# Two layers of a hybrid decoder: attention's output norm taken into the next head's first stage, and a projection dealt out between scores

## The reference

```
xn = rms_norm(x, norm_mix);  columns of every mixer = xn @ w_in
A retention        S_t = gamma_h S + k v;          o = q S
B gated recurrence S_t = diag(f_t) S + k v;        o = S q      (f per channel)
C delta rule       S_t = g (I - beta k k') S + beta k v
D differential attention over the prompt, or over a paged cache + 8 tokens
o_A..o_C = head_rms_norm(o) * silu(gate)
o_D      = head_rms_norm(o) * (1 - lam_init)
h = x + (sum_b sigmoid(G_b xn) * (o_b @ W_b)) @ w_out
y = h + product-key experts(rms_norm(h))
```

## Time and profile before

| | us |
|---|---|
| median of 3 runs | 6727.6 (6712.52 to 6736.32) |
| the profiled execution | 6737.32 |
| its span | 6735.6 |
| PE busy | 6265.5 (93%) |
| DVE busy | 3591.6 (53%) |
| ACT busy | 2141.3 (32%) |
| granted TensorE clock, mean | 0.958 |

### The profile page before, as it was taken

How to read it: one execution, slowest core, us unless ns; L and a number is a source line. 1 busy time by engine, 2 the same in 40 slices (tenths; PEclk the granted TensorE clock), 3 DMA queues, 4 the chain that set the end, 5 groups by cost and what they waited for, 6 DMA issues and landing times. The chain is left out here.

```text
span 6735.6 us, 109246 instructions
## 1 busy us (share of the span) xinstructions
PE 6265.5 (93%) x42728; PEld 5868.9 (87%) x42728; DVE 3591.6 (53%) x6661; ACT 2141.3 (32%) x3172; POOL 0.7 (0%) x6
## 2 busy tenths in 40 slices
PE   8998988979999989999989989889799999899999
PEld 6776768979999989999967767689799999899999
DVE  3444353337778865555434443533377888655554
ACT  2333333222234442222223333332222344422222
POOL 0000000000000000000000000000000000000000
PEclk9999988989999999999999999889899999999999
DMA  2212112224346655444322121122243466554543
GB/s 101 65 49 75 56 42 73 84 88 120 113 130 188 182 187 195 167 178 166 135 88 67 48 75 56 44 73 82 88 123 114 128 187 187 186 193 166 179 165 136
DMA packets 494389, 804.29 MB, mean 119 GB/s; under 512 B 81652, under 2 KB 302836, under 8 KB 475892
## 3 DMA queue, kind: packets, MB, share of 16 engines
q1 hardware_dynamic: 494116, 800.67, 37.4%
HBM read 616.20 MB, written 186.72 MB: 119 GB/s over the span
## 5 line engine op out<-in xcount | busy, mean ns | idle before, releaser
L1625 PE MATMUL ps<-xh,wh 128*128 128x288 f32 x4608 | 1376.5, 299 | 44.3 <-DVE wl L1841 44.3
L1625 PE MATMUL ps<-xl,wh 128*128 128x288 f32 x4608 | 1361.9, 296 | 0.0
L1625 PE MATMUL ps<-xh,wl 128*128 128x288 f32 x4608 | 1357.1, 295 | 0.0
L2041 PE MATMUL ps<-gh,vh 128*128 128x320 f32 (+1 forms) x4096 | 894.9, 300 | 73.2 <-DVE vl L2106 73.2
L1625 PEld LDWEIGHTS ps<-xh,wh 128*128 128x128 f32 x4608 | 867.2, 188 | 47.5 <-DVE wl L1841 45.2
L2041 PE MATMUL ps<-gl,vh 128*128 128x320 f32 (+1 forms) x4096 | 884.6, 298 | 0.0
L2041 PE MATMUL ps<-gh,vl 128*128 128x320 f32 (+1 forms) x4096 | 884.3, 297 | 0.0
L1625 PEld LDWEIGHTS ps<-xh,wl 128*128 128x128 f32 x4608 | 868.4, 188 | 0.0
L1625 PEld LDWEIGHTS ps<-xl,wh 128*128 128x128 f32 x4608 | 867.2, 188 | 0.0
L2106 DVE TENSOR_TENSOR vl<-vr,vh 128x512 fp32r<-128x512 f32 x512 | 353.2, 690 | 690.3 <-ACT vh L2061 690.0
L2041 PEld LDWEIGHTS ps<-gh,vh 128*128 128x128 f32 x4096 | 634.6, 191 | 86.2 <-issue 74.3
(11 more groups left out here) (374 smaller groups left out, 9175.7 us busy)
## 6 DMA issues: line engine op xcount, KB each, us to landing
raw<-in_u SPq DMA_DIRECT2D x256, 512.0 KB, 4.0
vr<-in_v SPq DMA_DIRECT2D x512, 256.0 KB, 2.9
activated<-go SPq DMA_DIRECT2D x256, 288.0 KB, 4.3
coefficients<-wt SPq DMA_DIRECT2D x36, 2048.0 KB, 9.3
gb<-activated SPq DMA_DIRECT2D x64, 1152.0 KB, 5.9
wb<-coefficients SPq DMA_DIRECT2D x64, 1152.0 KB, 8.3
wr<-in_w_cm SPq DMA_DIRECT2D x104, 512.0 KB, 4.5
wm<-in_w_merge SPq DMA_DIRECT2D x32, 768.0 KB, 4.2
```

The costliest lines, as they stand in the source:

```text
L1625: last = nc.tensor.matmul(out, wp[:, slot, k, :], xp[:, k, cols], start=(k == 0 and wp is T.wh and xp is T.xh), stop=(k == KD - 1 and wp i ...
L2041: last = nc.tensor.matmul(out, vp[:, x % 4, m * P:(m + 1) * P], gp[:, row, col:col + size], start=begins, stop=False, skip_group_check=True)
```

## The change

In words:

- `attention_stage` of heads 0, 1 and 2 no longer has the sum of squares, the root and the multiplication. ACT writes the square of the output to `T.late_sq` and then copies the output to `T.late` (both new tiles in SBUF), and the stage ends there. Head 3 keeps the old order.
- `retention_stage` of heads 1, 2 and 3 gets this work. PE sums the squares into banks 2 and 3 before anything else, and it waits for `late_mean` before the state products, which write those banks. ACT makes Ln and Exp before it takes unit 0. DVE multiplies `T.late` by gain and root into the branch buffer between `sc_ready` and the state updates.
- `hgrn_stage`, all heads: unit 4 goes into PE's queue as two halves, ahead of the scores of tiles 2 and 3. Unit 5 goes as four quarters: one ahead of the scores of tile 4, one after the transposes, one after the wait for the last mask and one after the state products. Unit 5 now uses bank 5 instead of bank 1, so PE waits for `taken` 6 before the outputs. The test whether the bank is free stands before the first part of a unit alone.

```diff
@@ -151,17 +151,19 @@
 FIRST_SLOTS = ((0, 1), (1, 1), (2, 1))
 
 
-def pe_ahead(nc, pe, T, s, slots, u, b, banks=1):
+def pe_ahead(nc, pe, T, s, slots, u, b, banks=1, first=0, count=KD):
     c, a = divmod(u, 2)
     slot, loads = slots[c]
-    if a == 0 and loads:
-        pe.wait_ge(s["w"][slot], 16 * loads)
-    if u >= banks:
-        pe.wait_ge(s["taken"], u - banks + 1)
-    for k in range(KD):
+    if first == 0:
+        if a == 0 and loads:
+            pe.wait_ge(s["w"][slot], 16 * loads)
+        if u >= banks:
+            pe.wait_ge(s["taken"], u - banks + 1)
+    for k in range(first, first + count):
         last = nc.tensor.matmul(bank(T, b)[:, 0:HALF], T.wr[:, slot, k, :], T.xn[:, k, a * HALF:(a + 1) * HALF],
                                 start=(k == 0), stop=(k == KD - 1))
-    last.then_inc(s["ahead"], 1)
+    if first + count == KD:
+        last.then_inc(s["ahead"], 1)
 
 
 def load_tile(sp, T, s, l, h, column, slot, after=0):
@@ -475,12 +477,12 @@
     sp.dma_start(T.s_in[:], state[l, :, h].rearrange("s k v -> k s v")).then_inc(s["s_loaded"], 16)
 
 
-def retention_stage(nc, T, l, h, slot):
+def retention_stage(nc, T, l, h, slot, late_slot):
 
     q, k, g = T.ret
     hq, hf, hg, hneg = T.hgrn
     qd = T.wk[:, 2, :]
-    with stage(nc, *W_SEMS, *AHEAD, "small_in", "scored", "turned", "sc_ready", *FINISH, *STATES) as (block, s):
+    with stage(nc, *W_SEMS, *AHEAD, "small_in", "late_sum", "late_mean", "late_root", "scored", "turned", "sc_ready", *FINISH, *STATES) as (block, s):
         s["w"] = [s["w0"], s["w1"], s["w2"], s["w3"]]
 
         @block.sync
@@ -494,6 +496,8 @@
 
         @block.tensor
         def _(pe):
+            if late_slot is not None:
+                wide_product(nc, T, 2, lambda k: T.ones, lambda k: T.late_sq, 1).then_inc(s["late_sum"], 1)
             for t in range(TILES):
                 last = nc.tensor.matmul(tile(bank(T, 4, NP_), t), tile(k, t), tile(q, t), start=True, stop=True)
             last.then_inc(s["scored"], 1)
@@ -501,6 +505,8 @@
                 last = nc.tensor.transpose(tile(bank(T, 6, NP_), t), tile(k, t), T.ident)
             last.then_inc(s["turned"], 1)
             pe_ahead(nc, pe, T, s, HGRN_SLOTS, 0, 1)
+            if late_slot is not None:
+                pe.wait_ge(s["late_mean"], 1)
             pe_state_products(nc, pe, T, s, lambda t: T.vt[:, t, 0:P])
             pe_ahead(nc, pe, T, s, HGRN_SLOTS, 1, 1)
             pe.wait_ge(s["sc_ready"], 1)
@@ -523,6 +529,11 @@
                 else:
                     act_take(nc, act, T, s, u, b, hg, ACT.Silu)
 
+            if late_slot is not None:
+                act.wait_ge(s["late_sum"], 1)
+                nc.scalar.activation(T.rs, halves(T, 2), ACT.Ln, bias=T.eps, scale=1.0 / P).then_inc(s["late_mean"], 1)
+                act.wait_ge(s["late_mean"], 1)
+                nc.scalar.activation(T.rs, T.rs, ACT.Exp, scale=-0.5).then_inc(s["late_root"], 1)
             take(0)
             take(1)
             act_square(nc, act, T, s)
@@ -541,6 +552,11 @@
                                     ALU.mult).then_inc(s["keys_ready"], 1)
             link(nc.vector.tensor_tensor(qd, q, T.hc[:, H_QD:H_QD + NP_], ALU.mult))
             nc.vector.tensor_tensor(T.sc, bank(T, 4, NP_), T.hc[:, H_RM:H_RM + NP_], ALU.mult).then_inc(s["sc_ready"], 1)
+            if late_slot is not None:
+                dve.wait_ge(s["late_root"], 1)
+                link(nc.vector.scalar_tensor_tensor(out=two(T.br[:, late_slot, :].rearrange("p a n -> p (a n)")),
+                                                    in0=two(T.late), scalar=T.cols[:, 8:9], in1=T.rs,
+                                                    op0=ALU.mult, op1=ALU.mult))
             dve_prompt_states(nc, dve, T, s, link, T.hc[:, H_GT:H_GT + TILES])
             dve_sample_states(nc, dve, T, s, link, T.hc[:, H_G8:H_G8 + DEC_B])
             dve.wait_ge(s["small_in"], 16)
@@ -608,6 +624,7 @@
                 n = 1 + (LEVELS if t < 4 else 3)
                 b = 2 * (t % 2)
                 if t >= 2:
+                    pe_ahead(nc, pe, T, s, GDN_SLOTS, 4 + t // 4, 4 + t // 4, 2, *((0, 4), (4, 4), (0, 2))[t - 2])
                     pe.wait_ge(s["masked_"], t - 1)
                 for i in range(n):
                     lhs, rhs = (ke[0], q) if i == 0 else (ke[i - 1], qf[i - 1])
@@ -617,10 +634,12 @@
             for t in range(TILES):
                 last = nc.tensor.transpose(tile(bank(T, 6, NP_), t), tile(ke[LEVELS if t < 4 else 3], t), T.ident)
             last.then_inc(s["turned"], 1)
-            pe_ahead(nc, pe, T, s, GDN_SLOTS, 4, 4, banks=2)
+            pe_ahead(nc, pe, T, s, GDN_SLOTS, 5, 5, 2, 2, 2)
             pe.wait_ge(s["masked_"], TILES)
+            pe_ahead(nc, pe, T, s, GDN_SLOTS, 5, 5, 2, 4, 2)
             pe_state_products(nc, pe, T, s, vt)
-            pe_ahead(nc, pe, T, s, GDN_SLOTS, 5, 1)
+            pe_ahead(nc, pe, T, s, GDN_SLOTS, 5, 5, 2, 6, 2)
+            pe.wait_ge(s["taken"], 6)
             pe.wait_ge(s["sc_ready"], TILES)
             pe.wait_ge(s["st_ready"], 1)
             pe.wait_ge(s["s_loaded"], 16)
@@ -633,7 +652,7 @@
         def _(act):
             act.wait_ge(s["lb_in"], 1)
             nc.scalar.activation(T.lb[:, 0:2], T.lb[:, 0:2], ACT.Exp).then_inc(s["lb_exp"], 1)
-            take = lambda u: act_take_gdn(nc, act, T, s, u, 4 + u % 2 if u < 5 else u % 2)
+            take = lambda u: act_take_gdn(nc, act, T, s, u, 4 + u % 2 if u < 6 else u % 2)
             for r in range(LEVELS):
                 act.wait_ge(s["level_v"], r + 1)
                 if r:
@@ -1262,7 +1281,8 @@
                                             at[:, i * NS + b * DEC_T:i * NS + (b + 1) * DEC_T], start=False,
                                             stop=(b == DEC_B - 1 and i == PAGES - 1))
             last.then_inc(s["o_ready"], 1)
-            pe_finish(nc, pe, T, s)
+            if not more:
+                pe_finish(nc, pe, T, s)
 
         @block.scalar
         def _(act):
@@ -1320,8 +1340,14 @@
             nc.scalar.copy(at[:, 0:PAGES * NS], bank(T, 2)[:, 0:PAGES * NS]).then_inc(s["s_at"], 1)
             nc.scalar.copy(at[0:NS, PAGES * NS:(PAGES + 1) * NS],
                            bank(T, 2)[0:NS, PAGES * NS:(PAGES + 1) * NS]).then_inc(s["s_at"], 1)
-            act_square(nc, act, T, s)
-            act_root(nc, act, T, s)
+            if more:
+                act.wait_ge(s["o_ready"], 1)
+                nc.scalar.activation(T.late_sq, bank(T, 4, N), ACT.Square)
+                nc.scalar.copy(T.late, bank(T, 4, N)).then_inc(s["o_squared"], 1)
+                act.wait_ge(s["o_squared"], 1)
+            else:
+                act_square(nc, act, T, s)
+                act_root(nc, act, T, s)
 
         @block.vector
         def _(dve):
@@ -1382,12 +1408,13 @@
             nc.vector.tensor_scalar(diag[0][0][:, 0:NS], dc[:, C_STK:C_STK + NS], sm(0, 0), None, ALU.mult
                                     ).then_inc(s["diag_ready"], 1)
             link(nc.vector.tensor_tensor(gain, T.ph[:, Q_DN:Q_DN + 1], T.pl[:, L_OL:L_OL + 1], ALU.mult))
-            dve_finish(nc, dve, T, s, link, gain, slot, None)
+            if not more:
+                dve_finish(nc, dve, T, s, link, gain, slot, None)
 
 
 def head(nc, T, l, h, more):
 
-    retention_stage(nc, T, l, h, br_slot(0, h))
+    retention_stage(nc, T, l, h, br_slot(0, h), br_slot(3, h - 1) if h else None)
     hgrn_stage(nc, T, l, h, br_slot(1, h))
     gdn_stage(nc, T, l, h, br_slot(2, h), more)
     attention_stage(nc, T, l, h, br_slot(3, h), more)
@@ -2197,6 +2224,8 @@
                     T.ph = sb(sub, "ph", [P, PH_W])
                     T.vt = sb(sub, "vt", [P, TILES, 3 * P])
                     T.st = sb(sub, "st", [P, 5, P])
+                    late = sb(sub, "late", [P, 2, N])
+                    T.late, T.late_sq = late[:, 0, :], late[:, 1, :]
                     T.s_in = sb(sub, "s_in", [P, DEC_B, P])
                     T.s_new = sb(sub, "s_new", [P, DEC_B, P])
                     T.kt = sb(sub, "kt", [P, TILES, P])
```

## The result

The changed kernel took 6678.47 us, the median of four runs (6672.0 to 6690.07), and the kernel before 6730.46 beside it (6712.52 to 6736.32). The ratio is 0.993, with a 95% interval of 0.9918 to 0.9942; it is worked out over the runs and is not the quotient of the two medians (0.9923). The forecast was 6685, so 43 us less than before, where 52 were measured. The profiled execution took 6679.22 us with a span of 6677.6.

A forecast was written before the change was run, and what follows sets the result against it. PE was taken as the bound, with a serial chain at attention's end and DVE's masking ahead of the recurrence's keys copy. The norm move's 26 us plus the dealt units' 17 gave 43 less, 6685 us, range 6662 to 6708.

The forecast's parts named there:

- Part 1, the chain: Attention's end, six transitions: removing the path from square to barrier saves 5.3 us per transition.
- the sum of squares at 1.0 us: Retention's start: PE's added sum of squares costs only its full-clock time, 1.0 us per transition; the high end is 1.9.
- Nothing on PE but its order: Eight recurrence stages: no PE work is added or removed; 12 of unit 5's 16 instructions move into PE's pauses.
- DVE not delayed: Recurrence: scores of tiles 2 and 3 still reach DVE in time, with margins of 0.8 and 0.6 us.
- Part 2 at full clock, 9.3 us: Recurrence: the stretch from the keys' copy to the square shrinks from 11.60 to 9.3 us at full clock.
- 38 us without falls: Recurrence: gain if the clock held in all eight stages, 74 us against 112.5 from keys' copy to square.
- Falls, 2.5 of 8 at 8.3 us each: Recurrence: two or three of eight stages lose PE's clock, each costing 8.3 us, leaving 17 us of gain.
- The clock held in all eight: Rival, recurrence: split idle time never costs the clock; gain 64 us, so 6664; chance 0.13.
- Retention paid: Rival: sum of squares stays at low clock and DVE's multiplication is exposed; whole gain 32, so 6696; chance 0.09.
- the 1.9 of the rival: Retention: price in us of PE's sum of squares per transition if it stays at the low clock throughout.
- Eight falls: Rival's extreme, recurrence: the clock is lost in every stage; 8 us slower, so 6736; chance 0.03.
- scores were late: Rival, recurrence: scores of tiles 2 and 3 reach DVE late; 1 us late leaves 35, so 6693; chance 0.05.

The follow-up runs named there:

- experiment 4: Changed kernel with the last quarter of unit 5 also ahead of the state products: 6660.0 us, ratio 0.9902 to the kernel before.
- experiment 6: Changed kernel with three unused products in the entry stage of each layer, meant to start all heads 1.5 us later: 6675.32 us, one run.
- Part 1 alone: Kernel before with only attention's norm move, the recurrence keeping its old order: 6710.31 us, ratio 0.9971 to the kernel before.
- experiment 3: Changed kernel with two unused products in each of PE's two pauses before the state products: 6659.55 us, ratio 0.9905 to the kernel before.
- experiment 9: Changed kernel with four unused products at the end of attention of heads 0 to 2: 6679.08 us, ratio 0.9931 to the kernel before.
- Experiment 5: Changed kernel run once more with no edit: 6675.84 us, ratio 0.9918 to the kernel before.
- experiment 8: On experiment 4's kernel, the next head's first recurrence unit moved from retention into PE's waits at attention's end: 6638.34 us, ratio 0.987 to the kernel before.
- experiment 10: On experiment 8's kernel, the recurrence's sum of squares halfway through unit 6 and ACT's root before units 6 and 7: 6633.79 us, ratio 0.9858 to the kernel before.

## Why the prediction was right, and where it was not

- *Part 1, the chain.* Forecast 5.3 us per transition; the timeline shows 7.83 before and 2.08 after, 5.75. Right, and a little small: the copy overlaps the square by 0.1 us, and from the copy's end to PE's first product it is 0.9 us where 1.14 was taken.
- *Part 1, the sum of squares at 1.0 us.* About right: per head with the late norm retention is 1.07 us longer with the move alone, 0.5 in the profile of the changed kernel, where the clock came back 0.8 us sooner than before, and 1.4 in experiments 4 and 6. The state products did not wait for Ln, and DVE's multiplication stayed hidden with 1.71 us to spare. Part 1 alone is 30 us in the two stages of one profiled execution (26 forecast) and 15 in the median of ten runs. The profiled execution is the second fastest of the ten, whose spread is 27 us; what the slower ones lost was not profiled.
- *"Nothing on PE but its order", DVE not delayed.* Right in every trace.
- *Part 2 at full clock, 9.3 us.* Right (9.45), and 38 us without falls is 37 in experiment 3. The pauses were forecast at 1.3 and 1.1 us and are 1.47 and 0.81. Head 3 escaped the forecast, which had 2.66 us of pause for all: there it was 3.05 before, and both its stages fell; after, it is 1.84.
- *Falls, 2.5 of 8 at 8.3 us each.* This term was mis-sized for the profiled execution: four falls at 9.5, so 38 us in place of 21. Over the six profiled executions with this order of units it was 4, 3, 1, 1, 1 and 2, so 2.0 of 8. The chance was well sized, the price some 13% too low. Head 0 against head 1 shows where: state products 0.9 and 1.8 us more and last quarter 1.0, as forecast, but outputs 3.3 in place of 2.8 (they were priced with 0.21 us for a product of 128 columns, where the row at L498 gives 2.48 / 10 = 0.25), and unit 6 2.4 where 8.3 in all had left it 1.9.
- *What the forecast had no term for* is the clock in stages that were not edited: attention's middle and its sample outputs (some 14 of the 48 us there), the delta rule and the rest (13.5 us). In this execution it made up for the falls. In experiments 4 and 9 it took a gain back. The forecast's 43 and the measured 52 agree because these two misses have opposite signs, and that was luck. The second execution of the changed kernel has one fall less and 10 us more in attention, and ends at the same time. What fixes the clock in the middle of attention in one execution and not in the other stays open. Experiment 5 shows that part of the pattern changes with no edit at all.
- *The rivals.* The clock held in all eight only with unused products or more real work in the pauses. Retention paid 0.5 to 1.4 us per head on the mean, never the 1.9 of the rival. Eight falls never came. No scores were late.

The Trainium skill (TensorE: Matmul & The Clock Gate, "HAM oscillation — how this bites in real kernels") ties the loss of the clock to pauses longer than any in the recurrence. Its rule would have given 6664. The traces disagree: the clock fell over pauses of 1.47 and 0.81 us with one quarter of work between, and in none of eight stages with them filled (experiment 3).

## What to carry to other kernels

Work that is dealt into an engine's pauses pays twice where the pauses cost TensorE its clock, if it fills enough of them. Three quarters of the unit left 2.3 us of pause, and the clock fell in 12 of 48 stages profiled; the whole unit left 1.3 us, and it fell in 2 of 24 (experiments 4, 8 and 10). Price every block that is taken out of a long stretch also at the low clock, since it may be what brings the clock back: with the whole unit behind the pause the clock stayed low for 6.8 to 10.2 us, with a quarter of it for 20.5. Where the clock goes up and down, judge a part by the stage it touches and over several executions, since falls come and go in stages nobody edited, and between two executions of one kernel.

## What the runs showed of the hardware that I had not expected

- The same program loses the clock at other places in another execution: 4 and 3 falls in two profiles of one kernel, attention stages of 48.6 and 52.6 us with the same instructions.
- One run with 5 us of useless work before the heads took 6653.35 us, against 6679.22 in the changed kernel's profiled execution. It had one fall in place of four.
- The clock can fall while PE's row is full. In the changed kernel's head 0, 32 sample outputs of 8 columns follow each other from 314.93 to 319.38 with PE busy throughout, after a last pause of 0.46 us that ended at 314.57, and the clock goes low 2.8 us into them:

```profile
314.93:317.70 2.77, 2.77 (x26) 2.77 (x25) 0.00 (x0) 0.00 (x0) 0.00 (x0) 1.00 0.00 0
...
317.80:319.38 1.58, 1.57 (x8) 1.48 (x7) 0.00 (x0) 0.00 (x0) 0.00 (x0) 0.50 0.00 0
```
